# Expert weights issued earlier, a router tile evicted first, and two expert pairs whose rows stay on the chip: a hybrid attention and mixture-of-experts layer

## What is computed

```python
def hier_moe(h, w_r1, b_r1, w_r2, b_r2, w_gate, w_up, w_down):
    ...
    pg_top, g = lax.top_k(pg, 1)
    ...
    pe, e_local = lax.top_k(pf, TOP_K_INNER)
    weights = pg_top * pe / jnp.sum(pe, axis=-1, keepdims=True)
    eid = g * EXPERTS_PER_GROUP + e_local
    ...
    for e in range(N_EXPERTS):
        a = jax.nn.silu(t @ w_gate[e]) * (t @ w_up[e])
        y = y + combine[:, e:e + 1] * (a @ w_down[e])
...
    h = layer_norm(DEEPNORM_ALPHA * h + mix, ln1_g[l], ln1_b[l])
    ffn = hier_moe(h, ...)
    h = layer_norm(DEEPNORM_ALPHA * h + ffn, ln2_g[l], ln2_b[l])
```

## Time and profile before

| | |
|---|---|
| runs | 616.8, 593.65, 613.6 us; median 613.6 |
| profiled execution | 593.69 us |
| its span, first to last instruction | 592.0 us |
| its mean granted TensorE clock | 0.925 of full |
| TensorE busy | 499.4 us, 84% |
| VectorE, ScalarE, GpSimd busy | 229.1, 149.7, 161.9 us |
| DMA | 148.29 MB, mean 251 GB/s |

### The profile page before, as it was taken

The page is one execution under the profiler, slowest core; times in us unless marked ns, Lnnn a source line. Parts: engine busy times, 40 slices in busy tenths (PEclk is TensorE's granted clock), DMA queues, the critical chain, the costliest instruction groups (busy, mean ns, idle before and its releaser), DMA issues.

```text
span 592.0 us, 6141 instructions
## 1 busy us (share of the span) xinstructions
PE 499.4 (84%) x2182; PEld 283.7 (48%) x2182; DVE 229.1 (39%) x554; ACT 149.7 (25%) x311; POOL 161.9 (27%) x159
## 2 busy tenths in 40 slices
PE   5999999999799999999547799999786789777490
PEld 4586675856454556888443333333232333332130
DVE  2101482898789751255740211111111110102287
ACT  3233323522246664012410111111111111011032
POOL 2243332387624762033521011211111110101000
PEclk9999999999899999999757899999799998889875
DMA  9844458103029101990757799999999999998613
GB/s 321 298 50 51 51 164 259 38 1 142 1 92 356 52 1 37 389 389 38 276 222 270 303 396 418 422 417 419 421 421 419 422 419 419 422 420 329 237 78 142
DMA packets 42583, 148.29 MB, mean 251 GB/s; under 512 B 11362, under 2 KB 15970, under 8 KB 30264
## 3 DMA queue, kind: packets, MB, share of 16 engines
q1 hardware_dynamic: 37992, 139.71, 62.5%
q0 software_dynamic: 4464, 8.10, 3.7%
q10 hardware_dynamic: 96, 0.08, 0.0%
HBM read 137.16 MB, written 18.87 MB: 264 GB/s over the span
## 4 chain that ended last, share of the span: by engine, by line
PE 54%; DMA 20%; SPq 9%; DVE 7%; issue 5%; POOL 2%; ACT 2%; POOLq 0%; DVEq 0%; ACTq 0%
PE bank L1295 17%; DMA wgu<-in_w_up_dram 10%; PE bank L1460 8%; PE bank L1400 7%; DMA xe<-h_rows,row_from 6%; SPq L486 6%; PE bank L1268 3%; PE bank L1484 3%; PE bank L1362 3%; PE bank L1340 3%; SPq L489 3%; DMA y_rows<-ye,row_to 2%; PE bank L1315 2%; PE bank L1353 2%; PE bank L1446 1%
## 5 line engine op out<-in xcount | busy, mean ns | idle before, releaser
L1460 PE MATMUL bank<-wgu,xeT 128*64 128x512 f32 x512 | 127.9, 657 | 28.0 <-DMA wgu<-in_w_up_dram 27.2
L1460 PEld LDWEIGHTS bank<-wgu,xeT 128*64 128x64 f32 x512 | 42.6, 151 | 102.3 <-issue 100.1
L705 POOL DMA_INDIRECT y_rows<-ye,row_to x15 | 15.1, 1006 | 189.0 <-PE bank L1446 120.0
L1484 PE MATMUL bank<-wd,actT 128*64 128x512 f32 x256 | 60.7, 617 | 1.4 <-ACT actT L859 1.4
L1129 DVE TENSOR_TENSOR act_row<-bank,sil 128x256 f32<-128x256 f32 x16 | 6.8, 425 | 130.3 <-ACT sil L852 130.3
L607 POOL TENSOR_TENSOR ring_low<-ring,wt_high 128x1024 fp32r<-128x1024 f32 x12 | 28.6, 2384 | 55.4 <-ACT wt_high L732 55.4
L852 ACT ACTIVATE sil<-bank 128x256 f32<-128x256 f32 x16 | 6.1, 384 | 138.7 <-PE bank L1460 138.7
L1484 PEld LDWEIGHTS bank<-wd,actT 128*64 128x64 f32 x256 | 20.6, 142 | 37.6 <-issue 37.6
L1295 PE MATMUL bank<-xT_high,ring_low 128*128 128x512 f32 x128 | 32.7, 397 | 0.0
L1143 DVE COPY xeT<-bank 128x512 f32<-128x512 f32 x16 | 11.1, 692 | 54.6 <-PE bank L1446 54.6
L1340 PE MATMUL bank<-kT,qT 64*128 64x128 f32 (+3 forms) x64 | 26.0, 487 | 5.1 <-DVE nmx L995 4.3
(11 more groups left out here) (202 smaller groups left out, 761.8 us busy)
## 6 DMA issues: line engine op xcount, KB each, us to landing
wgu<-in_w_gate_dram SPq DMA_DIRECT2D x32, 1024.0 KB, 23.2
wgu<-in_w_up_dram SPq DMA_DIRECT2D x32, 1024.0 KB, 27.7
wd<-in_w_down_dram SPq DMA_DIRECT2D x32, 1024.0 KB, 28.5
ring<-in_w_in_dram SPq DMA_DIRECT2D x5, 2048.0 KB, 13.1
wo<-in_w_out_dram SPq DMA_DIRECT2D x2, 2048.0 KB, 7.9
y_rows<-zero SPq DMA_DIRECT2D x1, 4096.0 KB, 21.8
yg<-y_rows SPq DMA_DIRECT2D x8, 512.0 KB, 6.6
bias_rows<-brow SPq DMA_DIRECT2D x1, 2560.0 KB
```

The lines of the kernel that those rows point to most:

```text
L1460: ins = pe.matmul(bank[2 + i][half_rows(n), :], xeT[i][:, k, half_rows(n)], wgu[slots[n]][:, :, k, :], start=k == 0, stop=k == KD - 1)
L1484: ins = pe.matmul(bank[4 + c][half_rows(n), :], actT[i][:, m, half_rows(n)], wd[PAIR_SLOTS[p % 3][n]][:, m, 512 * c:512 * c + 512], start= ...
```

## The change

Four edits.

- SyncE no longer waits for the first gather before it issues the loads of expert 5.
- On VectorE `transposed_h(NT - 1)` goes ahead of `place` of tiles 0 to 2.
- The rows of pair 14 are kept on the chip too (KEPT = 2, STORED = 14). There are two tiles ye, used in turn, and `y_out` of a pair waits for the scatter of two pairs before. place_w and placeT are made for pairs 14 and 15 in the loop, at pairs 4 and 5 (PLACE), in PSUM banks 6 and 7. TensorE multiplies pair 14's rows for tiles 0 and 1 ahead of the last `gate_up`, and the rest at the end. The yg loads wait for 14 scatters, and stand ahead of the branch.
- ScalarE runs one Sqrt on a dummy value after its last `y_out`.

```diff
@@ sync @@
             load_down(4, PAIR_SLOTS[2][0], down_in_slot[PAIR_SLOTS[2][0]])
-            sp.wait_ge(gathered[0], 16)
             load_expert(5)
...
             sp.dma_start(b2[:, :], ln2_b[0].partition_broadcast(P)).then_inc(ln2_in, 16)
+            for i in range(2):
+                sp.wait_ge(y_stored[i], 16 * (STORED // 2))
+            for t in range(NT):
+                for c in range(2):
+                    sp.dma_start(yg[t][c][:, :], y_dram[SEQ * c + P * t:SEQ * c + P * t + P, :]).then_inc(y_gathered[t], 16)
             sp.wait_ge(y_ps, 2 * LAST)
...
-            sp.wait_ge(y_stored, 16 * LAST)
-            for t in range(NT):
-                for c in range(2):
-                    sp.dma_start(yg[t][c][:, :], y_dram[SEQ * c + P * t:SEQ * c + P * t + P, :]).then_inc(y_gathered[t], 16)
@@ gpsimd @@
-            for p in range(LAST):
+            for p in range(STORED):
@@ scalar @@
             def y_out(p):
                 act.wait_ge(y_ps, 2 * p + 2)
-                if p:
-                    act.wait_ge(y_stored, 16 * p)
-                act.activation(ye[:, 512:], bank[5][:, :], ACT.Copy).then_inc(y_hi, 1)
+                if p >= 2:
+                    act.wait_ge(y_stored[p % 2], 16 * (p // 2))
+                act.activation(ye[p % 2][:, 512:], bank[5][:, :], ACT.Copy).then_inc(y_hi, 1)
...
                 act_out(p + 1)
+                if 0 <= p - PLACE < KEPT:
+                    act.wait_ge(placeT_ps, p - PLACE + 1)
+                    act.activation(placeT[:, p - PLACE, :, :], bank[6 + p % 2][:, :].rearrange("p (t s) -> p t s", t=NT), ACT.Copy).then_inc(placeT_ready, 1)
...
             y_out(LAST)
+            act.activation(probe[:, :], eps_t[:, :], ACT.Sqrt)
@@ vector @@
+            transposed_h(NT - 1)
             dve.wait_ge(rank_ps, 1)
             place(0, NT - 1, bank[3][:, 0:NE * (NT - 1)])
-            transposed_h(NT - 1)
             route(NT - 1)
...
             for p in range(LAST - 1):
+                if 0 <= p - PLACE < KEPT:
+                    q = p - PLACE
+                    if q:
+                        dve.wait_ge(placeT_ps, q)
+                    for t in range(NT):
+                        for e in range(2):
+                            ins = dve.tensor_scalar(place_w[:, t, e, :], iota_r[:, :], last_rank[:, 0, t, 2 * q + e:2 * q + e + 1],
+                                                    last_wt[:, 0, t, 2 * q + e:2 * q + e + 1], ALU.is_equal, ALU.mult)
+                    ins.then_inc(place_ready, 1)
                 rows_out(p + 2)
@@ tensor @@
                 down(p)
+                if 0 <= p - PLACE < KEPT:
+                    pe.wait_ge(place_ready, p - PLACE + 1)
+                    for t in range(NT):
+                        ins = pe.transpose(bank[6 + p % 2][:, P * t:P * t + P], place_w[:, t, :, :].rearrange("p n s -> p (n s)"), ident[:, :])
+                    ins.then_inc(placeT_ps, 1)
+                if 0 <= p - PLACE - 1 < KEPT:
+                    pe.wait_ge(placeT_ready, p - PLACE)
                 transpose_act(p + 1)
...
+            for t in range(2):
+                place_rows(t, STORED)
             gate_up(LAST)
             transpose_act(LAST)
             down(LAST)
-            pe.wait_ge(placeT_ready, 1)
-            for t in range(NT):
-                for c in range(2):
-                    pe.wait_ge((y_lo, y_hi)[c], PAIRS)
-                    pe.matmul(bank[LAST_BANKS[t][c]][:, :], placeT[:, t, :], ye[:, 512 * c:512 * c + 512], start=True, stop=True).then_inc(last_ps, 1)
+            for t in range(2):
+                place_rows(t, LAST)
+            for t in range(2, NT):
+                place_rows(t, STORED)
+                place_rows(t, LAST)
```

More of the change, by code:

```diff
@@ L61 @@
 LAST = PAIRS - 1
+KEPT = 2
+STORED = PAIRS - KEPT
+PLACE = 4
 PAIR_SLOTS = ((2, 3), (1, 0), (4, 5))
@@ L144, in layer_kernel @@
         square = at("square", SLOT + 16 * KB, [D])
-        place_w = at("place_w", SLOT + 20 * KB, [NT, 2, CAP])
-        placeT = at("placeT", SLOT + 22 * KB, [NT, P])
         o_rowsT = at("o_rowsT", 5 * SLOT, [KD, SEQ])
@@ L166, in layer_kernel @@
         hT = [at(f"hT{i}", o + 4 * KB * i, [KD, P]) for i in range(2)]
-        ye = at("ye", o, [D])
+        ye = [at(f"ye{i}", o + 4 * KB * i, [D]) for i in range(2)]
         o += 8 * KB
@@ L175, in layer_kernel @@
                    [at("x_again1_0", o + 4 * KB, [D // 2]), at("x_again1_1", o + 10 * KB, [D // 2])]]
+        placeT = at("placeT", o, [KEPT, NT, P])
+        place_w = at("place_w", o + 10 * KB, [NT, 2, CAP])
         sil = [at(f"sil{i}", o + 4 * KB + KB * i, [DE]) for i in range(2)]
@@ L244, in layer_kernel @@
         eps_t = small("eps_t", [1])
-        last_rank, last_wt = at("last_rank", wpool_at, [2, NT, 2]), at("last_wt", wpool_at + 64, [2, NT, 2])
-        row_sum, neg_mean = at("row_sum", wpool_at + 128, [NT, 2]), at("neg_mean", wpool_at + 160, [NT])
-        square_sum, std2, rstd2 = [at(name, wpool_at + 192 + 32 * i, [NT]) for i, name in enumerate(("square_sum", "std2", "rstd2"))]
+        last_rank, last_wt = at("last_rank", wpool_at, [2, NT, 2 * KEPT]), at("last_wt", wpool_at + 128, [2, NT, 2 * KEPT])
+        row_sum, neg_mean = at("row_sum", wpool_at + 256, [NT, 2]), at("neg_mean", wpool_at + 288, [NT])
+        square_sum, std2, rstd2 = [at(name, wpool_at + 320 + 32 * i, [NT]) for i, name in enumerate(("square_sum", "std2", "rstd2"))]
         rank1 = small("rank1", [NT, NE])
@@ L366, in layer_kernel @@
         y_hi = sem("y_hi")
-        y_stored = sem("y_stored")
+        y_stored = [sem(f"y_stored{i}") for i in range(2)]
         y_gathered = [sem(f"y_gathered{t}") for t in range(NT)]
@@ L439, in layer_kernel @@
         SMALLS = 8 + NA
-        LAST_BANKS = ((0, 1), (2, 3), (6, 7), (4, 5))
+        LAST_BANKS = ((0, 1), (2, 6), (3, 7), (4, 5))
         block = ctx.enter_context(nc.Block())
@@ L705, in store_y @@
                 pool.indirect_dma_start(out=y_dram, out_offset=bass.IndirectOffsetOnAxis(ap=row_to[:, p:p + 1], axis=0),
-                                        in_=ye[:, :], in_offset=None,
-                                        bounds_check=2 * SEQ - 1, oob_is_err=False).then_inc(y_stored, 16)
+                                        in_=ye[p % 2][:, :], in_offset=None,
+                                        bounds_check=2 * SEQ - 1, oob_is_err=False).then_inc(y_stored[p % 2], 16)
             for p in range(3):
@@ L899, in _ @@
                         act.activation(o_sil[:, m, :], bank[m][:, :], ACT.Silu).then_inc(o_silu_ready, 1)
-            act.wait_ge(placeT_ps, 1)
-            act.activation(placeT[:, :, :], bank[0][:, :].rearrange("p (t s) -> p t s", t=NT), ACT.Copy).then_inc(placeT_ready, 1)
             silu(LAST)
@@ L1132, in y_out @@
                 dve.wait_ge(y_ps, 2 * p + 1)
-                if p:
-                    dve.wait_ge(y_stored, 16 * p)
-                dve.tensor_copy(ye[:, 0:512], bank[4][:, :]).then_inc(y_lo, 1)
+                if p >= 2:
+                    dve.wait_ge(y_stored[p % 2], 16 * (p // 2))
+                dve.tensor_copy(ye[p % 2][:, 0:512], bank[4][:, :]).then_inc(y_lo, 1)
             def rows_out(p):
@@ L1157, in _ @@
             for c in range(2):
-                link(dve.tensor_tensor(last_rank[:, c, :, :], hot[:, :, c, NE - 2:NE], rk[:, :, c:c + 1].to_broadcast([P, NT, 2]), ALU.mult))
-                link(dve.tensor_tensor(last_wt[:, c, :, :], hot[:, :, c, NE - 2:NE], wt[:, :, c:c + 1].to_broadcast([P, NT, 2]), ALU.mult))
+                link(dve.tensor_tensor(last_rank[:, c, :, :], hot[:, :, c, 2 * STORED:NE], rk[:, :, c:c + 1].to_broadcast([P, NT, 2 * KEPT]), ALU.mult))
+                link(dve.tensor_tensor(last_wt[:, c, :, :], hot[:, :, c, 2 * STORED:NE], wt[:, :, c:c + 1].to_broadcast([P, NT, 2 * KEPT]), ALU.mult))
             link(dve.tensor_tensor(last_rank[:, 0, :, :], last_rank[:, 0, :, :], last_rank[:, 1, :, :], ALU.add))
@@ L1533, in _, with place_rows @@
                         ins.then_inc(o_y_ps, 1)
+                pe.wait_ge(o_added, NE * NT + 1)
+            def place_rows(t, p):
+                for c in range(2):
+                    pe.wait_ge((y_lo, y_hi)[c], p + 1)
+                    ins = pe.matmul(bank[LAST_BANKS[t][c]][:, :], placeT[:, p - STORED, t, :], ye[p % 2][:, 512 * c:512 * c + 512],
+                                    start=p == STORED, stop=p == LAST)
+                    if p == LAST:
+                        ins.then_inc(last_ps, 1)
             pe.wait_ge(xeT_act, PAIRS)
             pe.wait_ge(xeT_dve, PAIRS)
[L1537 to L1540, removed]
+            for t in range(2):
+                place_rows(t, STORED)
             gate_up(LAST)
```

## The result

| | before | changed |
|---|---|---|
| runs, us | 616.8, 593.65, 613.6, 594.0, 616.46 | 589.63, 589.24, 589.77, 610.32, 590.7 |
| profiled execution, us | 593.69 | 589.63 |
| its span, us | 592.0 | 587.9 |
| mean granted TensorE clock | 0.925 | 0.933 |

The ratio of changed to before is 0.9941, 95% interval 0.9917 to 0.9966: 2 to 5 us faster, and within 2%. Both kernels have executions some 20 us longer than the rest, and the comparisons here leave those out, so the drop from the median 613.6 to the median 589.77 is not the effect of the change.

The account below looks back on a forecast made before the run. The prediction took weight loads saturating the DMA engines to bound the experts. Gains of 0.6 us before that stretch and 3.5 in the tail sum to 4.1 off the profiled 593.69: 589.6 us, range 581 to 611.

Parts of the forecast that it names:

- What bounds the kernel: Experts, about 340 to 544.8 us: weight loads saturate the DMA engines; only that stretch's start, bytes and what follows matter.
- Edit 1, worth 0 in bytes: Expert 5's loads without the wait: 3.15 MB moves between idle DMA places, gaining 0, but lands on the first gather.
- Edit 2, 4.7 earlier to the gather's issue: Router's end: evicting the last tile first starts `route` and issues the first gather 4.7 us earlier, at 304.7.
- The gather, 8.4, landing at 313.0: First gather, behind expert 5's loads: takes 8.4 us instead of 4.20, landing at 313.0, 0.6 before 313.62.
- All of it moves one for one with the landing of the first gather: From first gather to pair 4's loads: `gate_up` and load issues shift by as much as the gather's landing.
- the front's term of 0.6: Up to the saturated stretch: expert 5's early loads and the earlier eviction together gain 0.6 us.
- The tail, 3.5: End of kernel: yg loads leave 8.0 earlier, but queue behind the bias on two slow engines; first tile 3.5 us earlier.
- the 0.6 for pair 14's scatter: Tail: without pair 14's scatter the bias lands 0.6 us earlier, at 552.3 instead of 552.9.
- Edit 3 in the loop, 0: Expert loop up to 544.8: bytes unchanged, place matrices covered by queued loads, second ye only removes waits; 0.
- not held up: Rival on the tail: yg loads gain the full 8.0 us, with no queue in front; 585.1 us, chance 0.20.
- both are free: Rival: yg is not delayed and the first gather keeps its 4.2 us; 581.0 us, chance 0.10.
- served only behind expert 5: Rival: first gather waits out expert 5's loads, landing at 317.5; 594.1 us, chance 0.18 including any other loss.

Follow-up runs that it names:

- e4: Kernel before with only the last tile's eviction (`transposed_h(NT - 1)`) moved ahead of `place`; 588.6 us, ratio 0.9903.
- e1: Changed kernel with SyncE's wait for the first gather put back ahead of expert 5's loads; 585.1 us, ratio 0.9855.
- e7: e1 with VectorE's ten small instructions on routing weights moved behind `gated(0)`; 582.2 us, ratio 0.9799 to the kernel before.
- e5: Kernel before with only SyncE's wait for the first gather removed ahead of expert 5's loads; ratio 1.0002.
- e10: The kernel of e1 run once more, for a profile that starts level with the others; 584.44 us.
- e6: Changed kernel with expert 5's early loads and the earlier eviction undone, leaving kept rows, second ye and Sqrt; two comparable runs, 590.57 and 591.01 us.
- e3: Changed kernel with SyncE's yg loads issued ahead of the two norm loads; 587.5 us, ratio 0.9883 to the kernel before.
- e8: Changed kernel with the first-gather wait back, yg loads ahead of the norm's, and ten small VectorE instructions behind `gated(0)`; 579.7 us, ratio 0.9762.
- e9: Changed kernel with expert 5's three loads issued a second time after the first gather landed; 590.05 us, ratio 0.9932 to the kernel before.
- e2: Changed kernel with ranks placed ahead of the last tile's eviction again, expert 5 still loaded early; ratio 0.9934 to the kernel before.

## Why the prediction was right and where it was not

- *What bounds the kernel*: right. DMA share stayed 1.02, and e4, e1 and e7 moved the start of the saturated stretch and with it the end.
- *Edit 1, worth 0 in bytes*: right (e5, 1.0002).
- *Edit 2, 4.7 earlier to the gather's issue*: 4.9 counted from VectorE's last instruction ahead of the edit. The end of `place` stayed pinned to GpSimd's addition.
- *The gather, 8.4, landing at 313.0*: 8.78, landing at 312.46. e1 and e10 show that expert 5's loads are the cause.
- *"All of it moves one for one with the landing of the first gather"*: this step failed, and with it the front's term of 0.6. Landing and start of the first `gate_up` came 1.16 earlier, pair 4's loads 0.32 later. From the start of the first `gate_up` to the end of the second took 24.5 (315.30 to 339.80) for 23.0 (316.46 to 339.49): the two multiplications 2.4 longer, the pause and the transposes between them 1.0 shorter. The forecast took TensorE's durations as given. What the traces show in their place is the clock: it rose 5.6 us after the start of the first `gate_up`, where it had risen 2.9 after it, and fell inside the second one, where it had fallen ahead of it. Why it did is open. Over many executions the term can't be told from 0: the changed kernel gained 3.5 (2 to 5) and the tail alone, in the two runs of e6, 3.2.
- *The tail, 3.5*: 3.3 to the first tile, 4.0 to `add_last(0)`; the difference is a wait of 0.7 for TensorE that went. Counted from the last `gate_up`, which started 0.28 later, it is 3.6 and 4.2. The reason given, the norm's loads in front of yg on late DMA engines, is borne out by e3 and by the bias at 552.5 for 552.3. That just two engines are late is read from a mean share of 0.12; no run shows which. The sentence on engines 7 and 15 in the Trainium skill (DMA: Bandwidth & Descriptors, Latency and other measured facts) fits that number, but no run shows that it was these two. Two smaller terms: the 0.6 for pair 14's scatter has no row behind it, and the bias landed 0.4 earlier (552.5 for 552.9); and the last `down` was put 1.8 behind `gated`, where the rows of before give 1.4 (561.40 to 562.84). It came 1.5 behind it (558.09 to 559.55), and nothing hung on it.
- *Edit 3 in the loop, 0*: right; the saturated stretch from pair 4's loads to the last `gate_up` is 205.3 before and after (544.83 - 339.53, 545.11 - 339.85).
- *The rivals*: "not held up" and "both are free" fell with the gather's 8.78 and yg's 10.1, "served only behind expert 5" with the landing at 312.45, under the 317.5 it needed.
- *The number*: that 589.6 was met is luck in part. Against the profile of before, the front lost 0.3 where 0.6 was to be won, and from the last `gate_up` on 4.4 were won where 3.5 were forecast; the two misses of 0.9 cancel. And this profile was 0.86 ahead before the first edit, a head start that e6's does not have (its gather leaves at 309.58, before's at 309.42). If it is taken off, the front lost 1.2, and the sum is 3.2 and not 4.1; e6 has 3.2 too.
- *The time it is a gain from*: this failed too. The recorded forecast gives 589.6 as the time of the changed kernel while the runs on record had the median 613.6; so read, it is a gain of 24 us, which neither its own sum (4.1) nor the measured ratio (3.5, 2 to 5) supports. (Its text also has 609.5, from the median, and keeps to 589.6 because its rows are those of the profiled execution.) A forecast from one profiled execution has to be told as a difference from that execution. The upper end of 611 stretched the range for the same reason, and named no mechanism.

## What to carry to other kernels

A load moved from one idle place of the DMA engines to another gains nothing by its bytes, but it may meet the one small transfer that everything waits for: here 3 MB issued early doubled a gather of 4 us (8.78 for 4.12) and cancelled a gain of about 5 (585.1 us without the early issue, 589.8 with it). When the stream that follows is saturated, look for what starts it, down to ten instructions of 0.2 us, and keep bulk loads that are not urgent out of the queue ahead of the first gather and ahead of the loads that open the tail.

## What was not expected of the hardware

- The clock's rise to its upper level came at different moments of the same work. Counted from the start of the first `gate_up`, and read from the granted clock in steps of 0.5 us, it came after 2.9 (before), 3.2 (e4), 3.1 (e6), 3.1 (e10), 3.7 (e7), 3.4 (e8) and 2.7 (e9), all with 3 MB of loads beside it, and after 5.6 (changed), 5.4 (e2) and 5.5 (e3), where none of these did. The idle time ahead of it does not sort these (e2's gather landed as late as before the change, and e2 stands with the late ones). But e1, with loads, has 4.2, and e5, without, 3.9, and e9's total did not follow its earlier rise. Whether it goes with the transfers is open.
- A pause of TensorE of 3.48 us was followed by a fall of the clock, one of 1.41 at the same place was not (e10 and e7): 0.9 us less in the transposes and 0.6 in `gate_up`, on top of the pause itself. In the changed kernel, after the same pause of 3.48, the transposes still ran at the upper level (1.06) and the fall came 1.4 us behind the pause, inside the second `gate_up`, which took 8.71 for the 7.63 of e10.
